# Expert lookup by product keys: 352 tokens dense and 160 by gathers, in place of 384 and 128

## The reference

```python
def peer(h, w_query, sub_keys, expert_u, expert_v):
    ...
    s_top, i_top = lax.top_k(s, K)                    # K = 16 of 128 keys, twice per head
    ...
    best, pos = lax.top_k(cand, K)
    eidx = jnp.take_along_axis(cand_idx, pos, axis=-1)   # key1 * 128 + key2
    g = jax.nn.softmax(best, axis=-1)
    ...
        u = expert_u[ib]
        a = jax.nn.gelu(jnp.einsum('thkd,td->thk', u, xb).astype(jnp.float32), approximate=False)
        w = (gb * a).astype(expert_v.dtype)
        return jnp.einsum('thk,thkd->td', w, expert_v[ib])
```

## Time and profile before

| what | us |
|---|---|
| median of 3 runs | 2923.21 |
| the profiled execution's own time | 2918.37 |
| its span | 2916.7 |
| TensorE (PE) busy | 2691.5 (92%) |
| VectorE (DVE) busy | 2090.2 (72%) |
| ScalarE (ACT) busy | 1336.4 (46%) |
| GpSimd (POOL) busy | 676.5 (23%) |
| choosing, spreading | 506 to 609, 609 to 772 |
| experts, closing | 772 to 1717, 1717 to 1735 |

### The profile page before, as it was taken

One profiled execution on the slowest core, in us unless ns is written; L12 is line 12 of the kernel. 1 busy time (PEld: TensorE's weight loads), 2 busy tenths in 40 slices (PEclk: granted clock), 3 DMA queues, 4 the chain that ended last, 5 costly groups with the idle time before them and its releaser, 6 DMA issues. The chain is left out here.

```text
span 2916.7 us, 36219 instructions
## 1 busy us (share of the span) xinstructions
PE 2691.5 (92%) x12848; PEld 2203.1 (76%) x12848; DVE 2090.2 (72%) x3739; ACT 1336.4 (46%) x2079; POOL 676.5 (23%) x519
## 2 busy tenths in 40 slices
PE   4999989999899999999999969989899699999994
PEld 3666767567777999999999957867677588888883
DVE  4666567989778777777778766555534799988994
ACT  3225442246433333333333334442333588778883
POOL 2300023410133443434434411000000311222210
PEclk8999989999999999999999989999999799999997
DMA  7730011436699988888988932223221799999993
GB/s 233 269 106 1 30 60 66 150 143 236 256 329 330 318 291 295 281 291 306 308 308 304 314 120 89 87 79 108 84 96 39 255 405 379 369 373 371 366 360 131
DMA packets 268639, 651.65 MB, mean 223 GB/s; under 512 B 48580, under 2 KB 109764, under 8 KB 264904
## 3 DMA queue, kind: packets, MB, share of 16 engines
q1 hardware_dynamic: 218584, 481.96, 46.5%
q0 software_dynamic: 46448, 142.67, 14.7%
q10 hardware_dynamic: 3456, 25.17, 2.1%
HBM read 617.09 MB, written 57.74 MB: 231 GB/s over the span
## 5 line engine op out<-in xcount | busy, mean ns | idle before, releaser
L3217 ACT ACTIVATE ex_w_hi<-expert_raw 128x1024 fp32r<-128x1024 f32 x384 | 374.5, 1072 | 40.2 <-DMA expert_raw<-in_w 18.3
L1941 PE MATMUL bank<-v_hi,peer_w_hi 128*128 128x512 f32 x768 | 300.4, 391 | 10.5 <-DVE peer_w_lo L2047 7.5
L3263 DVE TENSOR_TENSOR ex_w_lo<-expert_raw,ex_w_hi 128x1024 fp32r<-128x1024 f32 x256 | 296.0, 1217 | 7.8 <-ACT ex_w_hi L3217 6.5
L1941 PE MATMUL bank<-v_hi,peer_w_lo 128*128 128x512 f32 x768 | 300.3, 391 | 0.0
L1941 PE MATMUL bank<-v_lo,peer_w_hi 128*128 128x512 f32 x768 | 300.2, 391 | 0.0
L1989 ACT ACTIVATE v_hi<-v_in 128x1024 fp32r<-128x1024 f32 x128 | 130.4, 1054 | 344.5 <-PE bank L1941 312.0
L1916 POOL DMA_INDIRECT got_rows<-in_u_rows,diff x128 | 195.6, 1528 | 300.5 <-DVE got_rows L2014 262.7
L1929 PE MATMUL bank<-h_hi,u_hi 128*128 128x384 f32 x768 | 258.1, 336 | 0.8 <-DVE u_lo L2007 0.8
L1929 PE MATMUL bank<-h_hi,u_lo 128*128 128x384 f32 x768 | 257.9, 336 | 0.0
L1929 PE MATMUL bank<-h_lo,u_hi 128*128 128x384 f32 x768 | 257.6, 335 | 0.0
L1916 POOL DMA_INDIRECT got_rows<-in_expert_v,diff x128 | 182.6, 1426 | 244.2 <-DVE peer_acc L2019 204.1
(11 more groups left out here) (516 smaller groups left out, 6204.6 us busy)
## 6 DMA issues: line engine op xcount, KB each, us to landing
expert_raw<-in_w SPq DMA_DIRECT2D x384, 512.0 KB, 7.7
v_in<-in_expert_v SPq DMA_DIRECT2D x128, 512.0 KB, 6.6
u_in<-in_u_tiles SPq DMA_DIRECT2D x96, 512.0 KB, 4.5
ada_in<-in_w_ada SPq DMA_DIRECT2D x48, 512.0 KB, 5.1
gates_by_key<-spread ACTq DMA_DIRECT2D x24, 1024.0 KB, 9.7
gate_in<-gates_by_key SPq DMA_DIRECT2D x384, 64.0 KB
ring<-in_w_in SPq DMA_DIRECT2D x11, 2048.0 KB, 8.3
early_u<-in_u_tiles SPq DMA_DIRECT2D x32, 512.0 KB, 3.9
```

Of the source, the lines that this page charges most:

```text
L1941: last = pe.matmul(g.bank[2 + o][:, :], x[:, par, e, i * P:(i + 1) * P], v[par][:, e, c], start=(first and n == 0), stop=(final and n == 3 ...
L3217: act.activation(hi[kind][:, c, :], raw_piece(raw, u * PIECES + c), ACT.Copy).then_inc(s["r_hi"], 1)
L3263: dve.tensor_tensor(lo[which][:, c, :], raw_piece(raw, u * PIECES + c), hi[which][:, c, :].bitcast(F32), ALU.subtract).then_inc(s["r_lo"], 1)
```

## The change

`DENSE_T` becomes 352: two full tiles and 96 tokens of the third. The dense products have 352 columns; the third tile of w is padded with zeros to 128, so `down` keeps its six groups. The last 32 tokens of the third tile are "shared": four partitions work on one of them, each on a quarter (32) of its 128 picks. So `ROWS` = 128 + 32 = 160 gathers for u and as many for v; `h_rows` and `acc` get a second part, and `close_first` adds the four partial sums to the third tile's banks with two matmuls by a 0/1 matrix `fold`. The lists of the shared picks are brought to their partitions by six small matmuls with a shifted identity (`move`) at the end of `choose_experts`. One early key moves from spreading (11) to choosing (19). Spreading has 88 groups, and a last gate block of 32 tokens in a tensor of its own. The transposes that make `h_rows` move from the opening of `experts` into spreading. `HALFWAY` becomes step 37.

```diff
-DENSE_T = 3 * P
+SHARED = 32
+PARTS = P // SHARED
+OWN = P - SHARED
+FULL_TILES = 2
+DENSE_T = FULL_TILES * P + OWN
 ROWS_TILE = 3
 PICKS = PH * TOPK
-EARLY_RANKING, EARLY_BEFORE, EARLY_CHOOSING, EARLY_SPREADING = 2, 6, 20, 12
+PART = PICKS // PARTS
+ROWS = PICKS + PART
+EARLY_RANKING, EARLY_BEFORE, EARLY_CHOOSING, EARLY_SPREADING = 2, 6, 21, 11
@@ choose_experts, gpsimd at the start, vector and tensor at the end
+                pool.memset(move[:, :], 0.0).then_inc(s["h_clear"], 1)
+                pool.wait_ge(s["h_clear"], 1)
+                pool.tensor_copy(move[:, OWN - SHARED:OWN], g.ident[:, OWN:P]).then_inc(s["h_move"], 1)
...
+                dve.scalar_tensor_tensor(shared_at[:, :], key[:, 0, FULL_TILES].rearrange("p h k -> p (h k)"), float(PK),
+                                         key[:, 1, FULL_TILES].rearrange("p h k -> p (h k)"), ALU.mult, ALU.add).then_inc(s["h_shared"], 1)
...
+                dve.wait_ge(s["h_shared"], 1)
+                dve.tensor_copy(rows_at[OWN:P, PICKS:ROWS], shared_at[OWN:P, PICKS - PART:PICKS])
+                dve.tensor_copy(rows_gate[OWN:P, PICKS:ROWS], shared_gate[OWN:P, PICKS - PART:PICKS])
+                dve.wait_ge(s["h_moved"], 1)
+                dve.tensor_copy(rows_at[0:OWN, PICKS:ROWS], g.bank[3][0:OWN, 0:PART])
+                dve.tensor_copy(rows_gate[0:OWN, PICKS:ROWS], g.bank[4][0:OWN, 0:PART])
...
+                for b, src in ((3, shared_at), (4, shared_gate)):
+                    for j in range(PARTS - 1):
+                        at = OWN - SHARED - j * SHARED
+                        last = pe.matmul(g.bank[b][0:OWN, 0:PART], move[:, at:at + OWN], src[:, j * PART:(j + 1) * PART],
+                                         start=(j == 0), stop=(j == PARTS - 2))
+                last.then_inc(s["h_moved"], 1)
@@ spread_gates
+BLOCKS = [GB] * (DENSE_T // GB) + [DENSE_T % GB]
+LAST_GB = BLOCKS[-1]
...
+        twice = opening.v_in[:, 0, :].rearrange("p (k t) -> p k t", t=P)
...
+            def flip(pe, b):
+                if b == 2:
+                    pe.wait_ge(s["i_twice"], 1)
+                if b >= 2:
+                    pe.wait_ge(s["i_hrows"], b - 1)
+                for k in range(4):
+                    at = b % 2 * 4 + k
+                    rows = g.ht[:, at, ROWS_TILE * P:T] if b < 2 else twice[:, at, :]
+                    last = pe.transpose(g.bank[6 + b % 2][:, k * P:(k + 1) * P], rows, g.ident[:, :])
+                last.then_inc(s["i_flip"], 1)
...
+                    if n % FLIPS_A_GROUP == FLIPS_A_GROUP // 2 and n // FLIPS_A_GROUP < 4:
+                        flip(pe, n // FLIPS_A_GROUP)
...
+                act.activation(twice.rearrange("p k (n t) -> p k n t", t=SHARED),
+                               g.ht[:, :, DENSE_T:DENSE_T + SHARED].unsqueeze(2).to_broadcast([P, DC, PARTS, SHARED]), ACT.Copy).then_inc(s["i_twice"], 1)
...
+                sp.wait_ge(s["i_flip"], 4)
+                for e in range(KEYS_A_STEP):
+                    sp.dma_start(opening.v_in[:, e, :], g.a["expert_v"][0, e * P:(e + 1) * P, :]).then_inc(opening.v_loaded[e], 16)
@@ experts
-    HALFWAY = EQ + (Q - EQ) * 6 // 13
+    HALFWAY = EQ + (Q - EQ) * 9 // 20
...
-            return 2 * EQ - (-(PICKS - 2 * EQ) * (q - EQ + 1) // (HALFWAY - EQ))
-        return PICKS - (-PICKS * (q - HALFWAY + 1) // (Q - HALFWAY))
+            return 2 * EQ - (-(ROWS - 2 * EQ) * (q - EQ + 1) // (HALFWAY - EQ))
+        return ROWS - (-ROWS * (q - HALFWAY + 1) // (Q - HALFWAY))
...
-                    for b in range(NB):
+                    for b in range(NB - 1):
                         sp.dma_start(gate_in[:, q % 2, b], gates[b, :, q * GT:(q + 1) * GT, :]).then_inc(s[f"j_g{q % 2}"], 16)
+                    sp.dma_start(gate_last[:, q % 2], last_gate[:, q * GT:(q + 1) * GT, :]).then_inc(s[f"j_g{q % 2}"], 16)
...
-                for n in range(2 * PICKS):
+                for n in range(2 * ROWS):
...
-                for b in range(2):
-                    for k in range(4):
-                        last = pe.transpose(g.bank[2 + b][:, k * P:(k + 1) * P], g.ht[:, 4 * b + k, DENSE_T:T], g.ident[:, :])
-                    last.then_inc(s["j_flip"], 1)
                 up(pe, EQ, True)
                 up(pe, EQ + 1)
-                pe.wait_ge(s["j_hrows"], 2)
+                pe.wait_ge(s["j_pad"], 2)
...
-                        dve.tensor_tensor(w[:, e, :].rearrange("p (b t) -> p b t", t=GB), (gel_in[:, q % 2, e, :] if q < EQ else gel[:, e, :]).rearrange("p (b t) -> p b t", t=GB),
-                                          gate_in[:, q % 2, :, e, :], ALU.mult).then_inc(s["j_w"], 1)
+                        gelu = gel_in[:, q % 2, e, :] if q < EQ else gel[:, e, :]
+                        dve.tensor_tensor(w[:, e, 0:WHOLE_T].rearrange("p (b t) -> p b t", t=GB), gelu[:, 0:WHOLE_T].rearrange("p (b t) -> p b t", t=GB),
+                                          gate_in[:, q % 2, :, e, :], ALU.mult).then_inc(s["j_wfront"], 1)
+                        dve.tensor_tensor(w[:, e, WHOLE_T:DENSE_T], gelu[:, WHOLE_T:DENSE_T], gate_last[:, q % 2, e, :], ALU.mult).then_inc(s["j_w"], 1)
@@ close_first
+            @block.tensor
+            def _(pe):
+                for c in range(2):
+                    pe.matmul(g.bank[2 + 2 * FULL_TILES + c][:, :], fold[:, :], acc[:, 1, c * BANK:(c + 1) * BANK], start=False, stop=True).then_inc(s["k_fold"], 1)
```

More of the change, by code:

```diff
@@ L1583, in choose_experts @@
         wide = [P, PH, TOPK, TOPK]
-        with stage(nc, "h_sums h_dve h_chain h_top h_shift h_exp h_gate h_keyed h_red h_hit h_mul h_flipped h_out h_iota" + MemoryRows.SEMS) as (block, s):
+        shared_gate = gate[:, FULL_TILES].rearrange("p h k -> p (h k)")
+        with stage(nc, "h_sums h_dve h_chain h_top h_shift h_exp h_gate h_keyed h_red h_hit h_mul h_flipped h_out h_iota h_shared h_moved h_clear h_move" + MemoryRows.SEMS) as (block, s):
             memory = MemoryRows(g, ctx, s, mem_t)
@@ L1735, in spread_gates @@
         one2 = sb("one2", [P, SLOTS, GT4, P])
-        out = sb("spread", [P, 2, P, GB])
-        with stage(nc, "i_one1 i_one2 i_mm i_out i_hhi i_uhi i_ulo" + EarlyUp.SEMS) as (block, s):
+        out = sb("spread", [P, 2, P * GB])
+        twice = opening.v_in[:, 0, :].rearrange("p (k t) -> p k t", t=P)
+        with stage(nc, "i_one1 i_one2 i_mm i_out i_hhi i_uhi i_ulo i_twice i_flip i_hrows i_clear i_fold" + EarlyUp.SEMS) as (block, s):
             early = EarlyUp(g, ctx, {**s, "y_st0": opening.gel_stored[0], "y_st1": opening.gel_stored[1]}, EARLY_CHOOSING, (4, 5), early_gel)
@@ L1742, in _ @@
             def _(dve):
-                for n in range(NB * GQ):
+                for n in range(GROUPS):
                     if n >= SLOTS:
@@ L1801, in _ @@
             def _(sp):
[L1802 removed]
                 early.load(sp, 0)
                 early.load(sp, 1)
[L1805 to L1812 removed]
+                for n in range(EARLY_SPREADING):
+                    if 1 <= n and n + 1 < EARLY_SPREADING:
+                        early.load(sp, n + 1)
+                    if n >= 1:
+                        early.keep(sp, n - 1)
+                    if n in (3, 5):
+                        e = (n - 3) // 2
                         sp.dma_start(opening.u_in[:, e, :], g.a["u_tiles"][EARLY + e].rearrange("p c e -> p (c e)")).then_inc(opening.u_loaded[e], 16)
[L1814 to L1816 removed]
+                sp.wait_ge(s["i_flip"], 4)
+                for e in range(KEYS_A_STEP):
+                    sp.dma_start(opening.v_in[:, e, :], g.a["expert_v"][0, e * P:(e + 1) * P, :]).then_inc(opening.v_loaded[e], 16)
                 for e in range(KEYS_A_STEP):
@@ L1821, in _, with experts @@
                 sp.wait_ge(stored[0], STORED * (NB // 2))
-def experts(g, gates, early_gel, rows_at, rows_gate, acc, opening):
+def experts(g, gates, last_gate, early_gel, rows_at, rows_gate, acc, opening):
     nc, a = g.nc, g.a
@@ L1835, in experts @@
     AHEAD = 2
-    NB = DENSE_T // GB
-    HALFWAY = EQ + (Q - EQ) * 6 // 13
+    NB = len(BLOCKS)
+    WHOLE_T = DENSE_T - LAST_GB
+    HALFWAY = EQ + (Q - EQ) * 9 // 20
     def rows_done(q):
@@ L1941, in down @@
                             last = pe.matmul(g.bank[2 + o][:, :], x[:, par, e, i * P:(i + 1) * P], v[par][:, e, c],
-                                             start=(first and n == 0), stop=(final and n == 3 * GT - 1))
+                                             start=(first and n == 0), stop=(final and i < FULL_TILES and n == 3 * GT - 1))
                             n += 1
@@ L1978, in _ @@
             def _(act):
-                for b in range(2):
-                    act.wait_ge(s["j_flip"], b + 1)
-                    act.activation(h_rows[:, b * BANK:(b + 1) * BANK], g.bank[2 + b][:, :], ACT.Copy).then_inc(s["j_hrows"], 1)
                 for q in range(Q):
@@ L2052, in _, with close_first @@
                         dve_row(dve, n)
-def close_first(g, acc, gate):
+def close_first(g, acc, gate, fold):
     nc, a = g.nc, g.a
```

(12 more changed lines are left out.)

106 lines of the change are left out of this document (61 added, 45 removed).

## The result

The changed kernel took 2874.9 us (median of 4 runs, 2872.3 to 2883.9) beside 2922.3 for the kernel before: a ratio of 0.984, 95% interval 0.982 to 0.986. Forecast was 2878, range 2864 to 2904. Its profiled execution took 2874.4 us with a span of 2872.6.

What follows compares the result with a forecast made beforehand. VectorE was taken to bound spreading and TensorE the loop; -29.4 + 5 - 13 - 5 - 1.5 - 1 = -44.9 us gave 2873.5 from the profiled 2918.4, or 2878 by the median, range 2864 to 2904.

Steps and rivals of the forecast that it cites:

- Part 1: Loop of the experts stage: `up` products at 352 columns start every 0.160 us, period 15.91, -29.4 us over 46 steps.
- Rival (c): Products of 352 columns don't start earlier than those of 384, so -29.4 falls away, and the lag too: 2902 us; chance 0.04.
- Part 2: VectorE in the loop, 160 rows a half: about 4 us of lag vanish at the end; cost 0 to 1 us.
- Part 3: DMA queues in the loop: 361 GB/s wanted in the first half, 16.1 us a step there, 4 us of lag.
- rival (a): DMA queues limit the loop's first half, 16.9 us a step: +18 instead of +5, 2891 us, up to 2905; chance 0.24.
- (b): Queues in the loop no better than ordinary rates and filled only to 0.95: slower than before, +9, 2932 us; chance 0.04.
- Part 4: Spreading stage: 88 groups instead of 96 at 1.632 us each, nothing taken for the work moved in: -13 us.
- Part 5: Opening of `experts`: gates finish sooner with 2 MB less in the last block, first `down` after 18.5 us: -5 us.
- Part 6: Early steps of `experts`, paced by loads: 0.1 of 2.8 MB less, -1.5 us (bounds -5 and +3).
- Part 7: Ranking and choosing: early products save 3.4 us, later loads and moving the picks eat most: -1 us (bounds -4 and +2).

## Why the prediction was right, and where it was not

**Part 1 (-29.4): right.** `up` products start every 0.160 us, as worked out. The period fell by 0.693 instead of 0.64: 48 x 0.160 + 36 x 0.2267 is 15.84 of 15.853, so the 0.07 us that the old step had beyond its products is nearly gone as well; why, no run shows. Over 46 steps 31.9 us; 1.3 come back at the start of the loop, where TensorE waits 1.6 us for u_lo. The kernel with the columns alone gave 28.5 in the loop. Rival (c) is out.

**Part 2 (VectorE, 0 to 1): the mechanism right, the term too small.** The unstalled iteration of six rows was 16.15 by the sum and is 16.02. Timeline of VectorE:

```profile
1609.80 2.35 DVE L2093 TENSOR_TENSOR v_lo<-v_in,v_hi 128x1024 fp32r<-128x1024 f32 x2
1612.07 0.48 DVE L2110 TENSOR_TENSOR peer_w<-gel,gate_in 128x320 f32<-128x320 f32 x1
1612.47 0.18 DVE L2112 TENSOR_TENSOR peer_w<-gel,gate_last 128x32 f32<-128x32 f32 x1
...
1617.67 8.23 DVE L2085 SCALAR_TENSOR_TENSOR peer_acc<-got_rows,row_w,peer_acc 128x1024 f32<-128x1024 f32 x6
1625.82 2.35 DVE L2093 TENSOR_TENSOR v_lo<-v_in,v_hi 128x1024 fp32r<-128x1024 f32 x2
```

Its wait for u_hi is gone, as forecast. VectorE falls back 0.17 us a step; ACT, whose w_hi follows VectorE, reaches its wait for the buffer of v_hi later each time: 6.82 us of it in the middle of the first half, 3.06 at 1635. It costs the loop nothing. But I had set the 4.19 us that VectorE once waited before its last v_lo against the lag, and it was not enough: there is no wait before that v_lo now, and TensorE stands at the last step. Timeline of PE:

```profile
1661.28 0.50 PE L2012 MATMUL bank<-v_hi,peer_w_hi 128*128 128x512 f32 x1 [2.05 <-DVE peer_w_lo L2114]
```

That is +2.3 us (+4.1 in the other profile). The five kernels with fewer rows a step in the second half (switch at 36, or 128 rows) are all back at 16.5, so this wait is VectorE's lag. In the other profile it is 2.12 us, no longer. Its tail has 1.7 us more because the granted clock was lower in TensorE's last products. Windows of these products, first profile and second:

```profile
1661.00:1670.00 9.00, 8.45 (x36) 6.68 (x36) 6.55 (x6) 0.00 (x0) 0.00 (x0) 1.00 0.00 0
1671.60:1682.00 10.40, 10.08 (x36) 7.81 (x36) 6.38 (x6) 0.00 (x0) 0.00 (x0) 0.84 0.00 0
```

In the second the clock was at 1.2 GHz for 3.4 us right behind the wait. Why it fell there and not in the first profile, after nearly the same wait, no run shows; of the three further kernels with this second half unchanged one ended in 18.9 us and two in 20.5, with a clock of 1.00 and 0.84. That VectorE is next behind TensorE is shown by the repeated subtraction: 1.14 us more a step, 47 to 50 us slower. The 1 us counted for the turn, where ACT waits for the last dot product, is nothing in the trace: two v_hi releases 17.44 and 14.26 us apart are twice 15.85.

**Part 3 (the queues, +4): wrong, and it was the reason that I gave rival (a) 0.24.** The rate was forecast rightly, 361 GB/s in the first half and 347 in the second, where 346 was said; a window of the second half:

```profile
1290.00:1640.00 350.00, 350.00 (x1857) 318.99 (x1856) 310.24 (x351) 120.85 (x176) 179.95 (x130) 1.00 0.97 347
```

That it would be close to a ceiling was not so: 373 GB/s ran beside a TensorE busy to 100%, and 394 did too, once the loop's first two steps were over, in which the 4.4 us were lost. The failed step is the division of the bytes by what the queues moved per share of their busy time. That share is the time that packets were under way, and as it came out at 1.03 packets overlap in it; the quotient rose from 334 to 372 GB/s for the gathers when more was asked of them. The Trainium skill's figure of about 358 GB/s for a core (DMA: Bandwidth & Descriptors, Specifications), which is the half of 716 for two cores, is passed by 15 and 32 GB/s from 930 to 1230 us in these two runs, where one core works. Rivals (a) and (b) are out. Their sums took 8 us of lag off where Part 2 lets 4 vanish, and give no reason; with 4 they would stand at 2895 and 2936, which changes nothing here. Parts 2 and 3 together were +5 and measured about +3.6 (1.3 and 2.3): a term too small and one too large nearly made up for each other.

**Part 4 (-13): right,** -13.5 us; the transposes and copies that moved in are hidden.

**Part 5 (-5): too much,** -3.1 and -2.5 us. The first `down` came 20.4 and 21.0 us after the opening, where 18.5 was forecast. What ends last is as forecast, the last block's gates. Timelines of ACT's queue, POOL, VectorE and PE:

```profile
755.78 2.22 ACTq L1858 DMA_DIRECT2D last_gates_by_key<-spread  x4
```

```profile
768.14 1.07 POOL L1987 DMA_INDIRECT got_rows<-in_u_rows,diff  x1 [6.07 <-DMA last_gates_by_key<-spread]
```

```profile
776.32 0.49 DVE L2110 TENSOR_TENSOR peer_w<-gel_in,gate_in 128x320 f32<-128x320 f32 x1 [4.68 <-DMA gate_last<-last_gates_by_key]
779.81 0.57 PE L2012 MATMUL bank<-v_hi,peer_w_hi 128*128 128x512 f32 x1 [3.20 <-issue]
```

From the store to POOL's going on are 12.4 us, 16.1 before: 2 MB less of stores saved 3.8 us where I took 5, and as the store is issued 3.7 us ahead of the opening instead of 4.2, 3.2 are left of it. From POOL's row to the first `down` it is 11.6 us before and 11.7 after, so nothing came on top. The run with five gate loads in front opened after 17.7; its early steps took that back.

**Part 6 (-1.5)** came out at -2.5 and -1.5. But this stretch took from 140.1 to 144.8 us in kernels that do the same in it as the changed one, and 146.0 and 147.6 where the second step's gelu was late and the clock was low behind it; what makes the rest of its scatter is open. The bounds of -5 and +3 said as much.

**Part 7 (-1): +0.4.** The two copies behind the last transposes are there (VectorE at 609.28 and 609.38, the stage closing right behind). With 11 us of scatter ahead of this point the profiles don't separate -1 from +0.4.

The total agreed within 1 us because the errors were small and of both signs, not because every term was right: the loop and its tail gave 3.9 us more than forecast, and 2.9 that were lost in the unchanged stages behind took most of it back. That closeness is luck; the mechanisms of Parts 1, 2 and 4 are not.

## What to carry to other kernels

Before work is taken from the busiest engine, add up the unstalled iteration of the next one from its own rows: here VectorE's busy share was 0.89 in the second half and its step of 16.02 us was still longer than the new period, and what a share hides shows first where the loop ends. A DMA busy share of 0.99 does not say that no more bytes go through; add a load and see. A ring of n buffers carries n uses in a row without a wait, and no more where a fetch takes longer than they do; where a wait on a gather comes at every n+1st use, add a buffer before blaming the bandwidth, and where an opening is made shorter, look at which load of the next step is last in its queue.

## What the runs showed of the hardware

- One core kept 394 GB/s over 300 us (960 to 1260) with its 16 DMA engines, gathers of 4 KB rows and plain loads together, and TensorE was busy for all of it. From 930 to 1230 it was 390, 60.82 MB of it gathers, with single slices at 411.
- Float32r products with 128 rows start every 0.160 us at 352 columns, 0.1733 at 384 and 0.2267 at 512: 0.00042 us for each column more, in both steps, at a granted clock of 1.00.
- VectorE's product of 128x320 takes 0.48 us and that of 128x32 0.18 us, the pair 0.58 from start to end. By the slope between them one of 352 would take 0.51, so splitting it costs about 0.07 us (an estimate).
- TensorE's granted clock went to its lower level, 1.2 GHz, for 3.4 us after a wait of 2.12 us (end of the repeated changed kernel), for 6.8 us at one of 2.73 us (512 KB more a step), and for 10.2 us at ones of 6.77 and 7.51 us (gate loads first, seven buffers). After the wait of 2.05 us at the end of the first profile of the changed kernel it did not fall.
